# First experts' results written by slot and gathered per token; gate and up weights of a block's second half staged in two copies, one block ahead

## The reference, cut to what matters

```python
# first block: 32 experts, two per token
y = lax.map(expert_block, (x_pad, blk_expert)).reshape(P, D).astype(jnp.float32) * c_pad[:, None]
out = jax.ops.segment_sum(y, tok_pad, num_segments=T + 1)[:T]
# expert_block(xb, e): hb = silu(xb @ w_gate[e]) * (xb @ w_up[e]); return hb @ w_down[e]
h = h + hier_moe(rms_norm(h, norm_ffn_g[l]), ...)
# second block: 64 experts, eight per token, weighted and summed in the same way, plus a shared expert
```

## Time and profile before

| | us |
|---|---|
| median of 3 runs (3436.56 to 3442.18) | 3438.87 |
| the profiled execution, its own time | 3440.28 |
| its span, first to last instruction | 3438.6 |
| TensorE busy in it | 3131.8 (91%) |
| VectorE busy | 1557.3 (45%) |
| DMA, mean over the span | 164 GB/s |

### The profile page before, as it was taken

How to read it: one execution, slowest core, us unless ns; L and a number is a source line. 1 busy time by engine, 2 the same in 40 slices (tenths; PEclk the granted TensorE clock), 3 DMA queues, 4 the chain that set the end, 5 groups by cost and what they waited for, 6 DMA issues and landing times. The chain is left out here.

```text
span 3438.6 us, 46192 instructions
## 1 busy us (share of the span) xinstructions
PE 3131.8 (91%) x14927; PEld 1560.1 (45%) x14928; DVE 1557.3 (45%) x2429; ACT 727.9 (21%) x1169; POOL 625.3 (18%) x917
## 2 busy tenths in 40 slices
PE   8999989997999996789969998889899999999992
PEld 4444445544665444333337774444343334333430
DVE  3322234446775123434447765344444444444444
ACT  2222223343543010111114330221011111111112
POOL 1000000000000000233420000000344444444442
PEclk9999999998999997899969999999999999999996
DMA  6201021124121024799841011221788999988885
GB/s 231 98 30 43 0 86 49 49 74 95 50 78 71 25 112 171 271 385 383 293 155 37 24 30 59 77 97 43 274 285 281 360 331 307 316 287 284 282 268 178
DMA packets 180326, 564.84 MB, mean 164 GB/s; under 512 B 18684, under 2 KB 93024, under 8 KB 143072
## 3 DMA queue, kind: packets, MB, share of 16 engines
q1 hardware_dynamic: 142864, 429.69, 32.9%
q0 software_dynamic: 34128, 127.45, 14.7%
q10 hardware_dynamic: 3240, 6.45, 0.5%
HBM read 460.27 MB, written 103.27 MB: 164 GB/s over the span
## 5 line engine op out<-in xcount | busy, mean ns | idle before, releaser
L1894 PE MATMUL gu_ps<-w_gu,second 128*64 x1648 | 728.9, 595 | 11.7 <-DVE second L1992 8.5
L1897 PE MATMUL gu_ps<-h,second 128*64 128x512 f32 x1648 | 728.9, 595 | 0.0
L1894 PEld LDWEIGHTS gu_ps<-w_gu,second 128*64 128x64 f32 x1648 | 226.5, 138 | 476.9 <-issue 476.9
L1923 PE MATMUL y_ps<-w_dn,hid_t 128*64 x824 | 387.9, 615 | 30.4 <-DVE hid_t L1980 27.2
L1926 PE MATMUL y_ps<-second,hid_t 128*64 128x512 f32 x824 | 388.4, 615 | 0.0
L355 PE MATMUL front<-second,wcol 128*128 128x512 f32 x768 | 330.4, 592 | 4.8 <-ACTq L63 2.4
L1522 POOL COPY moe_idx<-moe_slot_tok 128x1 int32<-128x1 int32 x4 | 0.6, 183 | 1814.0 <-DVEq L1457 1226.4
L1843 POOL TENSOR_TENSOR idx_y<-moe_slot_tok,moe_side 128x1 int32<-128x1 int32 x103 | 201.1, 1953 | 576.7 <-ACT second L1953 576.7
L1967 DVE COPY h<-w_gu 128x4096 f32 x109 | 249.6, 2290 | 76.5 <-SPq L1771 71.1
L1974 DVE COPY second<-w_dn 128x2048 f32 x105 | 128.9, 1227 | 274.4 <-PE y_ps L1926 271.5
L355 PEld LDWEIGHTS front<-second,wcol 128*128 128x128 f32 x768 | 145.8, 190 | 188.5 <-issue 188.5
(11 more groups left out here) (453 smaller groups left out, 4570.5 us busy)
## 6 DMA issues: line engine op xcount, KB each, us to landing
w_gu<-in_w_gate_dram SPq DMA_DIRECT2D x96, 1024.0 KB, 12.7
w_gu<-in_w_up_dram SPq DMA_DIRECT2D x96, 1024.0 KB, 15.4
w_dn<-in_w_down_dram SPq DMA_DIRECT2D x96, 1024.0 KB, 10.6
wcol<-in_w_in_dram SPq DMA_DIRECT2D x12, 1024.0 KB, 5.4
qk_by_head<-stage SPq DMA_DIRECT2D x32, 384.0 KB, 3.7
qk<-qk_by_head SPq DMA_DIRECT2D x16, 768.0 KB
w_gu<-in_w_in_dram SPq DMA_DIRECT2D x20, 512.0 KB, 5.0
token_sums<-zero POOLq DMA_DIRECT2D x19, 512.0 KB, 12.7
```

Source lines behind the costliest of these rows:

```text
L1894: nc.tensor.matmul(gu_ps[0:PART, slot], x_t[:, slot, c, 0:PART], w_gu[:, bass.ds(ws, 1), :, c, :].rearrange("p o g n -> p (o g) n"), start ...
L1897: last = nc.tensor.matmul(gu_ps[PART:P, slot], x_t[:, slot, c, PART:P], st_gu[:, slot, :, c, :], start=c == 0, stop=c == C - 1)
L1923: nc.tensor.matmul(y_ps[0:PART, cs], hid_t[:, c, 0:PART], w_dn[:, bass.ds(ws, 1), c, cs].rearrange("p o n -> p (o n)"), start=c == 0, stop ...
```

## The change

- The first experts' results are no longer scaled by share nor added up in memory. ScalarE copies `y_ps` to `y` and itself issues a plain DMA of the 128 rows to their slots in a new table `expert_rows_1`. GpSimd's part shrinks to the gathers of the rows, which no longer carry shares (1024 columns, not 1056).
- `dispatch` of the first half makes no `dense` table; instead it keeps each token's two slots (`G.y_slot`) and, in the slots' order, its two shares (`G.y_share`).
- The residual rows stay in the SBUF buffer `second`; `merge` no longer writes them to memory.
- `take_sums`: GpSimd gathers for each tile of 128 tokens the two result rows (16 indirect DMAs), VectorE does two multiply-adds per tile onto the residual rows, TensorE turns them, ScalarE copies the columns.
- In both halves, the second half's gate and up weights are staged to one place, in two copies of half the size, one block ahead: VectorE's order in step i ends in gate/up staging of i+1, then down staging of i. TensorE waits for the first copy before a block's gate matmuls and for the second before their middle. The turned rows and the SiLU's output have one place each.
- The zero fills in `lru` are 9 of `token_sums` and 16 of `expert_rows_1`, where 18 of `token_sums` were.
- The numbers of weight slots, 5 and 4, stand in both versions.

```diff
@@ lru, GpSimd @@
-            zero_second(pool, sum_d, 1, zero[:, 0:D], zero_out)
+            zero_rows(pool, sum_d, S + P, T + 1, zero[:, 0:D], zero_out)
             pool.wait_ge(block_done, 2)
-            zero_second(pool, sum_d, 2, zero[:, 0:D], zero_out)
+            zero_rows(pool, y_d, S * K1, NB1 - S * K1 // P, zero[:, 0:D], zero_out)
@@ merge, SyncE @@
-                sp.wait_ge(o_taken, t + 1)
-                sp.dma_start(sum_d[t * P:(t + 1) * P, :], G.x2[:, t, :]).then_inc(sum_out, 16)
@@ take_sums @@
+        @block.gpsimd
+        def _(pool):
+            for t in range(T):
+                for k, (to, came) in enumerate(((near, near_in), (far, far_in))):
+                    nc.gpsimd.indirect_dma_start(to[:, t, :], None, y_d, bass.IndirectOffsetOnAxis(
+                        ap=G.y_slot[:, t, k:k + 1], axis=0)).then_inc(came[t], 16)
...
+        @block.scalar
+        def _(a):
+            for t in range(T):
+                a.wait_ge(turned, t + 1)
+                nc.scalar.activation(cols[:, :, t * P:(t + 1) * P], tp[:, t % 2], ACT.Copy).then_inc(taken, 1)
...
+            def add(t, k, of):
+                return d.scalar_tensor_tensor(out=rows[:, t, :], in0=of[:, t, :], scalar=G.y_share[:, t, k:k + 1],
+                                              in1=rows[:, t, :], op0=ALU.mult, op1=ALU.add)
+
+            for t in range(T):
+                v.wait_ge(near_in[t], 16)
+                add(t, 0, near).then_inc(part, 1)
+                v.wait_ge(far_in[t], 16)
+                v.wait_ge(part, t + 1)
+                add(t, 1, far).then_inc(added, 1)
@@ dispatch @@
-            pool.wait_ge(dense_out, 16)
+            if scores is not None:
+                pool.wait_ge(dense_out, 16)
...
+                st(d.tensor_copy(G.y_slot[:], slot[:]))
+                st(d.tensor_tensor(late[:, 0], G.e[:, :, 0], G.e[:, :, 1], ALU.is_gt))
...
@@ experts @@
-        st_gu = stage.rearrange("p t d -> p (t d)").rearrange("p (s g c n) -> p s g c n", s=2, g=2, c=C)
+        st_gu = stage[:, 0:4].rearrange("p t d -> p (t d)").rearrange("p (g c n) -> p g c n", g=2, c=C)
...
@@ experts, TensorE @@
-                pe.wait_ge(g_staged, i + 1)
+                pe.wait_ge(g_staged, 2 * i + 1)
...
                 for c in range(C):
-                    nc.tensor.matmul(gu_ps[0:PART, slot], x_t[:, slot, c, 0:PART],
+                    if c == C // 2:
+                        pe.wait_ge(g_staged, 2 * i + 2)
+                    nc.tensor.matmul(gu_ps[0:PART, slot], x_t[:, c, 0:PART],
...
@@ experts, ScalarE @@
+                    if by_slot:
+                        s.activation(y[:, 1 - slot, :], y_ps[:], ACT.Copy).then_inc(y_taken, 1)
+                        a.wait_ge(y_taken, 1 + i)
+                        to = out_d[i * P - P:i * P, :] if isinstance(i, int) else out_d[bass.ds(i * P - P, P), :]
+                        a.dma_start(to, y[:, 1 - slot, :]).then_inc(y_out[1 - slot], 16)
@@ experts, VectorE @@
-            def stage_gate_up(b, slot):
+            def stage_gate_up(b):
...
-                if not (isinstance(b, int) and b < 2):
-                    v.wait_ge(gu_ready, b - 1)
-                d.tensor_copy(st_gu[:, slot].rearrange("p g c n -> p (g c n)"),
-                              w_gu[:, bass.ds(e % W, 1)].rearrange("p o g c n -> p (o g c n)")).then_inc(g_staged, 1)
+                if not (isinstance(b, int) and b == 0):
+                    v.wait_ge(gu_ready, b)
+                ws = e % W
+                for h in range(2):
+                    cs = slice(h * (C // 2), (h + 1) * (C // 2))
+                    d.tensor_copy(st_gu[:, :, cs, :],
+                                  w_gu[:, bass.ds(ws, 1), :, cs, :].rearrange("p o g c n -> p (o g) c n")).then_inc(g_staged, 1)
...
+                stage_gate_up(i + 1)
                 stage_down(i)
-                stage_gate_up(i + 2, slot)
```

More of the change, by code:

```diff
@@ L270, in lru_load, with zero_rows, lru @@
         sp.dma_start(wgate[:, k], src[0]).then_inc(G.lru_wg, 16)
[L273 to L280, removed]
+def zero_rows(pool, to, first, tiles, zero, zero_out):
+    for t in range(tiles):
+        at = first + t * P
+        pool.dma_start(to[at:at + P, :], zero).then_inc(zero_out, 16)
+def lru(nc, A, G, spare, sum_d, y_d, wcol, wgate, w_low, ps):
     ph = phase(nc)
@@ L1260, in load_group, with take_sums @@
     sp.dma_start(G.w_head[:, g], w_in[:, :, at:at + P]).then_inc(G.w_head_in[g], 16)
-def take_sums(nc, A, G, sum_d, rows, cols):
+def take_sums(nc, A, G, y_d, rows, cols, near):
     ph = phase(nc)
     with ph.ctx:
-        other = ph.sb("other", [P, T, D])
+        far = ph.sb("far", [P, T, D])
         tp = ph.ps("tp", [P, 2, C, P])
-        turned, taken, added = ph.sems("turned taken added")
-        row_in = ph.sems(" ".join(f"row_in{t}" for t in range(T)))
+        turned, taken, added, part = ph.sems("turned taken added part")
+        near_in = ph.sems(" ".join(f"near_in{t}" for t in range(T)))
+        far_in = ph.sems(" ".join(f"far_in{t}" for t in range(T)))
         block = ph.ctx.enter_context(nc.Block())
+        @block.gpsimd
[4 more added lines that the diff above has]
+                        ap=G.y_slot[:, t, k:k + 1], axis=0)).then_inc(came[t], 16)
         @block.sync
         def _(sp):
-            for t in range(T):
-                sp.dma_start(rows[:, t, :], sum_d[t * P:(t + 1) * P, :]).then_inc(row_in[t], 16)
             for n in range(2):
                 load_head(sp, A, G, 0, n)
[L1280 to L1284, removed]
         @block.tensor
@@ L1716, in expert_state, with experts @@
     G.wd_v = wd_d.rearrange("l e (p c) n -> (l e) p (c n)", c=FC)
-def experts(nc, G, E, NB, W, rows_d, sum_d, loaded, stage, work, then=()):
+def experts(nc, G, E, NB, W, rows_d, out_d, loaded, stage, work, by_slot=False, then=()):
     ph = phase(nc)
@@ L2784, in program @@
             route1(nc, A, G, logits[:])
-            dispatch(nc, G, K1, E1, NB1, rows1_d, sum_d, 1)
-            experts(nc, G, E1, NB1, W1, rows1_d, sum_d, W1, first[:], second[:])
+            dispatch(nc, G, K1, E1, NB1, rows1_d)
+            with nc.sbuf_tensor("work_1", [P, 1, D], F32) as work:
+                experts(nc, G, E1, NB1, W1, rows1_d, y1_d, W1, first[:], work[:], by_slot=True)
         with ExitStack() as moe:
```

147 lines of the change are left out of this document (79 added, 68 removed).

## The result

| | before | after |
|---|---|---|
| median of the runs, us | 3439.65 (3436.56 to 3442.18, 4 runs) | 3401.27 (3397.92 to 3404.00, 4 runs) |
| span of the profiled execution | 3438.6 | 3402.2 |

The ratio is 0.9887, 95% interval 0.9876 to 0.9899: faster by 38.4 us. Forecast: 27.3 us faster, 3411.6, range 3392 to 3430. The time is in the range; the sum was 11 us short (9 us in the spans of the two profiled executions).

What follows compares the result with a forecast made beforehand. First experts' blocks were taken to wait for weights on the DMA engines, second experts to be bound by TensorE. Terms -6 - 20 - 10.5 + 8 + 1.2 = -27.3 us gave 3411.6 us, range 3392 to 3430.

Steps and rivals of the forecast that it cites:

- Part 1: First dispatch: share columns, their DMA and GpSimd's wait go; -6 us (-3 to -7).
- Part 2: First experts' blocks: less DMA engine time per block, staging one block ahead; -20 us (-36 to -12).
- I take the middle: First experts: 0.90 us saved per block, 19 us in 21 blocks, between cases of 14 and 28 us.
- The second block's +1.2: Start of first experts: second block's gate matmuls wait for rows' copy, then a half copy of 1.23 us; +1.2 us.
- The tail's -2.1: Last block of first experts: hidden rows' copy no longer stands behind a staging for a block that doesn't exist; -2.1 us.
- Part 3: First experts' end: plain write replaces the scatter and its landing wait; -10.5 us (-6.5 to -11).
- the two cases: First experts' end: 4 us in all with GpSimd's register steps, or 8 if its drain stays 4 us long.
- Part 4: Reading the results: 16 row gathers replace 16 plain reads; 36.3 us taken, +8 us (+3 to +12).
- third rival: Reading the results: VectorE's multiply-adds hold GpSimd back; +9 us, 3421; chance 0.11.
- Part 5: Second experts: staging change costs steady blocks 0, the second block +1.2; +1.2 us (0 to +16).
- fourth rival: Second experts: half copy falls to the slow rate, 63 us, 3475; chance 0.05.
- first two rivals: First experts: all 35.9 us of stalls go, 3395, chance 0.12; or the DMA saving brings nothing, 3431, chance 0.07.

Runs made afterwards that it cites:

- the kernel with the columns kept: Changed kernel whose first dispatch again makes the expert-share columns, writes them to memory and has GpSimd wait for them; 3407.08 us, ratio 0.9904.
- the kernel with four edits: Changed kernel plus later fifth weight slot, first rows copied between halves, SyncE awaiting last results, next phase's weight loads after third tile's gather; 3403.11 us, ratio 0.9895.
- the table of four: Second to 24th SiLU, old/new staging: results added in memory 295.9/294.3 us, by slot 273.8/267.9; single-change kernels: new staging 3436.12, by slot 3417.83.

## Why the prediction was right, and where its numbers were off

**What bounds the kernel.** Right in the main: the first experts' blocks waited for DMA engine time. DMA time taken away gives 22.1 us alone, put back it takes 28.3, and the staging alone gives 1.6. VectorE's order is not without a part: it is worth 5.9 us once the DMA time is freed.

**Part 1.** -5.5 against -6, and the kernel with the columns kept costs 5.8 us as a whole, 4.6 of them in the dispatch. The prediction did not ask whether the stalls behind it would eat it; they don't.

**Part 2.** The mechanism was right, the term was mis-sized: 19 us where 28.0 came. Two steps made it so. The first is "I take the middle": the loaded pair of 3.96 us was split with the lone gather's 1.77 us. In the loaded stretch a gather takes 1.32 us and the write 1.29, so by difference the scattering add had cost about 3.96 - 1.32 = 2.64, and a block gained 1.35 us: 21 x 1.35 = 28.4, the prediction's upper case ("as the lone prices do", 28 us). Two gathers alone don't fill the engines between issue and landing, so their share overstates one; that sentence is an argument, no run measured it. The second is that the staging was given nothing, since "asking for weights later doesn't make them come sooner". With the old staging the freed time gave 22.1 us, 3 more than the sum and 6 less than 28.4; the new staging gave the other 5.9. So the sentence is nearly right for the old route (1.6 us) and wrong by 5.9 us for the new one, and the right price alone would not have given the measured time of the old staging. The second block's +1.2 measured +1.4. The tail's -2.1 measured -0.3: the hidden rows' copy does come sooner, 8.56 us behind the 24th SiLU before and 7.41 after (1698.13), but from there to the result copy it is 7.91 instead of 7.01 us. TensorE's result matmuls there start 1.2 us after the copy has ended, against 0.41 before; the changed end of its list has more waits and increments there, and the prediction left that list out. That these are the cause is read from the code; no run shows it.

**Part 3.** -8.6 against -10.5. GpSimd's drain stood at 2.1 us, between the 0 and 4 of the two cases. Letting SyncE wait for the landing took 1.7 us of it away, at 4.1 us.

**Part 4.** +3.4 against +8. The step that failed is the same price, 16 x 1.77: the gathers took 1.30 us each, 20.7 instead of 28.3 us, and with that the prediction's own sum comes to 31.8 where 31.7 was measured. "They hide under the gathers" is wrong as a mechanism, though not as a number: VectorE's 16 multiply-adds of 1.28 us run back to back from 1719.96 to 1740.74, and TensorE's next matmuls follow 3.9 us later (1744.66); the last gather was issued at 1732.79. From the first landing on, VectorE has as much to do as the DMA engines.

**The third rival** (multiply-adds hold GpSimd) was right as a mechanism and cost 0.4 us here. In the changed kernel:

```profile
1719.88 0.95 POOL L1277 DMA_INDIRECT far<-expert_rows,y_slot  x1 [0.30 <-issue]
1721.14 0.95 POOL L1277 DMA_INDIRECT w_dn<-expert_rows,y_slot  x1 [0.30 <-issue]
1722.39 1.08 POOL L1277 DMA_INDIRECT far<-expert_rows,y_slot  x1 [0.30 <-issue]
...
1719.96 1.28 DVE L1306 SCALAR_TENSOR_TENSOR second<-w_dn,y_share,second 128x1024 f32<-128x1024 f32 x1 [12.53 <-DMA w_dn<-expert_rows,y_slot]
1721.36 1.28 DVE L1306 SCALAR_TENSOR_TENSOR second<-far,y_share,second 128x1024 f32<-128x1024 f32 x1
```

The issue at 1719.88 began 0.08 us before the first multiply-add and kept its 0.95 us. The one at 1721.14 began 0.10 us before a multiply-add's end and kept it too; the next, 0.25 us before an end (1722.64), took 1.08 and ended 0.83 us after it: the same holding, of 0.1 us. An issue every 1.25 us and a multiply-add of 1.28 have fallen into step, so each issue begins just before VectorE finishes. The last of the 16 goes 19.2 us after the first, where 15 x 1.25 is 18.8. In the kernel with four edits the multiply-adds came one by one as rows landed, out of step, and the price was the 4.9 us that rival had put at 9.

**Part 5 and the fourth rival.** The half copies run at the fast rate, 1.22 us, the period is 11.83 us, TensorE is busy 99.99 in 100. The slack of 0.1 to 0.6 us measured 0.43. The phase came out 1.4 us shorter where +1.2 was forecast: the second SiLU comes 1.0 us later (27.85 instead of 26.87 us into the phase), but the 77 blocks behind it take 910.98 instead of 912.84 us, since the kernel before had a few late blocks there (by 0.7, 0.5 and 0.4 us) and the changed one has none. Why is open.

**The first two rivals.** The first (all 35.9 us go, 3395) is nearer in time than the forecast, but its mechanism is not what came: 7.9 us of stalls are left, and the stage is not bound by TensorE, since 28.3 us of added DMA time show in it in full. The second (nothing comes of the saving) falls with the table of four.

**The sum.** By the table it promised 9.0 us too little among the blocks, 4.6 in the reading and 2.6 in the second experts, and 4.4 us too much in the dispatch and at the two ends of the first experts; phases put at 0 came 2.6 us longer. That these errors partly cancel is luck.

**The rest.** The first mixer's +2.2 us has no part in the change: over 13 profiles of 12 kernels it is either 410.0 to 410.4 or 411.8 to 412.2 us, with either number of zero fills. Attention is 298.0 and 299.6 us in the two kernels that add in memory and 301.1 to 302.2 in all that go by slot. In the last 50 us of it the changed kernel shows a granted clock of 0.97 where the kernel before shows 1.00, and 0.80 against 0.84 in the first 50. What in the change would do that stays open.

## What to carry to other kernels

Price a transfer in the stretch where it will run, and take away from a loaded sum only prices from loaded stretches: the lone gather's 1.77 us was 1.30 to 1.32 under load, and that one row stands in both of the largest errors. Where a stage is bound by DMA time, a better order of waits only moves the stalls (1.6 us) until the time itself is freed (then 5.9), so the two can't be priced one by one. And two engines that hold each other up can fall into step and hide it: an edit that made the inputs land one by one cost 4.9 us with no work added.

## What the runs showed of the hardware

A scattering add of 512 KB took about 2.64 us of the 16 engines' time under load (an estimate: the loaded pair before, 3.96, less the loaded gather after, 1.32; 3.50 alone), twice the plain write's 1.29. GpSimd's issue of an indirect gather takes 0.95 us; where it began while a multiply-add with both tensors in SBUF was running, it lasted until at least 0.81 to 0.83 us after that multiply-add's end (up to 1.84 us in all), and where it began before the multiply-add it kept its 0.95 us. TensorE's transposes ran at 0.14 us each in a stream of 44 and at 0.24, with a granted clock of 0.53, after an idle time of 2.85 us behind them, so keeping it busy bought nothing past that gap. GpSimd's drain at a phase's end cost 2.1 us with all its transfers landed.
